# Modulation weights split between a merged first stage and the mLSTM: four blocks of 512 columns at the start, eight later

## The chip, the cores and the metric

One Trainium2 chip, one core of it. The metric is the device time of one execution in microseconds (us); 3 runs of the kernel before are given by their median. Lower is better. TensorE (PE) runs at one of two clock levels, 1.2 or 2.4 GHz; the profile gives the granted share (0.50 or 1.00, or a mean of them).

## What is computed

The reference is three transformer layers over 512 tokens of width 1024, all in fp32. Only the head of the first one matters here:

```python
mx = [t[:, None, :] for t in jnp.split(jax.nn.silu(c) @ w_ada[l] + b_ada[l], 6, axis=-1)]
mc = jnp.split(jax.nn.silu(c_ctx) @ w_ada[l] + b_ada[l], 6, axis=-1)
hx = _modulate(_rms_norm(x, g_pre_mix[l]), mx[0], mx[1])
hc = _modulate(_rms_norm(ctx, g_pre_mix[l]), mc[0], mc[1])
yx, yc = _token_mixer(hx, hc, w_in[l], b_in[l], ...)          # project_in, mLSTM, convolution, project_out
x = x + mx[2] * _rms_norm(yx, g_post_mix[l])
hx = _modulate(_rms_norm(x, g_pre_ffn[l]), mx[3], mx[4])
x = x + mx[5] * _rms_norm(_moe_ffn(hx, ...), g_post_ffn[l])
```

`w_ada` is 1024 x 6144, 24 MB. Its product with two vectors, silu(c) and silu(c_ctx), gives six modulation vectors of 1024 for each. The first two (4 of 12 blocks of 512 columns) are wanted before the token mixer, the other four (8 blocks) only behind it.

## The kernel before

The kernel is a row of stages, each an `nc.Block()` in which every engine has its own hand-written instruction stream, with semaphores between them; a barrier of all engines stands between stages. Buffers are opened and closed with the stages. The order is that of the code: no scheduler moves anything. All loads go through one hardware queue, issued by SyncE (SP).

`load_and_modulation` loads the small tensors, x (3 MB, tokens and context, 768 columns for each of 8 k-tiles) and the 12 blocks of `w_ada` (2 MB each) through two buffers. For a block, TensorE makes 8 matmuls (line 302) whose stationary operand is silu_c (128 x 2) and whose moving operand is 512 columns of the weights, so the result is a row of 2 x 512; ScalarE copies it (line 333), TensorE turns it into columns with 4 transposes (line 310), and VectorE adds the bias into `m.mod` (line 344). A fp32 matmul of the program is two MATMUL records in the trace, each with an LDWEIGHTS of its own; a transpose is one.

Then come `modulation_gain` (line 480), `rms_norm` (squares in line 381, mean by a matmul with a constant in line 402, root 384, reciprocal 410, scaling 416, shift 390), and `project_in`, whose SP stream issues the loads of `w_in` when the stage before it has ended (line 536).

`mlstm` has three parts. First VectorE and ScalarE make running sums of the gates, then TensorE spreads them over the partitions with `sel` (line 853, 8 rounds, K = 64 rows) and ScalarE copies them. Then come 16 units (4 heads x 4 tiles of 128 tokens), each with two directions. TensorE's order over a unit is: `qk` for the next unit (line 871), `turn` (transposes of the scores, line 882), `pv` of the previous direction (line 894), `turn`, `pv`. VectorE makes logits (805), the product with the decay (794) and the division (773 to 781). At the end VectorE normalizes over each head (826 to 838), and TensorE, which waits for that (`mixed`), turns the result (line 911).

```python
                for n in range(len(subs)):
                    if n % 2 == 0 and n // 2 + 1 < len(units):
                        qk(n // 2 + 1)
                    turn(n)
                    if n >= 1:
                        pv(n - 1)
```

Of the kernel before, what the change touches and what calls it, by code (L numbers as in the profile page):

```python
# [20 lines left out]
P = 128  # L21
D = 1024
# [240 lines left out]
        return stack, sb, sem  # L263


def load_and_modulation(m, d):

    nc, ps = m.nc, m.ps
    stack, sb, sem = m.open()
    N_AB = 6 * D // 512  # L270
    with stack:
        w = [sb(f"w_ada{s}", [P, KT, 512]) for s in range(2)]
        cs = sb("silu_c", [P, KT, 2])
        row = [sb(f"row{s}", [2, 512]) for s in range(2)]
        small_in, x_in, w_in = sem("small_in"), m.x_in, [sem("w_in0"), sem("w_in1")]
        silu_done, w_used, row_copied, turned, added, seen = (
            sem(s) for s in ("silu_done", "w_used", "row_copied", "turned", "added", "seen"))
        with nc.Block() as block:
            @block.sync
            def _(sp):  # L280
                sp.dma_start(m.vec[:], d["vec"]).then_inc(small_in, 16)
                for s in range(2):
                    sp.dma_start(w[s][:].rearrange("p k n -> p (k n)"), d["w_ada"][s]).then_inc(w_in[s], 16)
                sp.dma_start(m.const[:], d["const"]).then_inc(small_in, 16)
                sp.dma_start(m.rowv[:], d["rowv"]).then_inc(small_in, 16)
                sp.dma_start(m.x[:].rearrange("p k t -> p (k t)"), d["x"]).then_inc(x_in, 16)
                with sp.Fori(1, N_AB // 2) as g:
                    for s in range(2):
                        sp.wait_ge(w_used, 2 * g - 1 + s)
                        sp.dma_start(w[s][:].rearrange("p k n -> p (k n)"), d["w_ada"][2 * g + s]).then_inc(w_in[s], 16)  # L290
                sp.wait_ge(small_in, 48)
                sp.wait_ge(x_in, 16)

            @block.tensor
            def _(pe):
                ident = CONST.of(m.const, "ident")[0:2, 0:2]

                def product(n, s, loads):
                    pe.wait_ge(w_in[s], loads)
                    pe.wait_ge(row_copied, n + 1)  # L300
                    for k in range(KT):
                        mm = pe.matmul(ps[0:2, s, :], cs[:, k, :], w[s][:, k, :], start=(k == 0), stop=(k == KT - 1))
                    mm.then_inc(w_used, 1)

                def turn(n, s):
                    pe.wait_ge(row_copied, n + 3)
                    pe.wait_ge(added, n + 1)
                    pe.sem_inc(seen, 1)
                    for a in range(4):
                        mm = pe.transpose(ps[:, 2 + s, 2 * a:2 * a + 2], row[s][:, a * P:(a + 1) * P], ident)  # L310
                    mm.then_inc(turned, 1)

                pe.wait_ge(silu_done, 1)
                product(0, 0, 16)
                with pe.Fori(0, N_AB // 2 - 1) as g:
                    product(2 * g + 1, 1, 16 * g + 16)
                    turn(2 * g, 0)
                    product(2 * g + 2, 0, 16 * g + 32)
                    turn(2 * g + 1, 1)
                product(N_AB - 1, 1, 8 * N_AB)  # L320
                turn(N_AB - 2, 0)
                turn(N_AB - 1, 1)

            @block.scalar
            def _(act):
                act.wait_ge(small_in, 48)
                act.activation(cs[:].rearrange("p k c -> p (k c)"), VEC.of(m.vec, "c"), ACT.Silu).then_inc(silu_done, 1)
                act.sem_inc(row_copied, 2)
                with act.Fori(0, N_AB // 2) as g:
                    for s in range(2):  # L330
                        act.wait_ge(w_used, 2 * g + s + 1)
                        act.wait_ge(added, 2 * g + s + 1)
                        act.activation(row[s][:], ps[0:2, s, :], ACT.Copy).then_inc(row_copied, 1)

            @block.vector
            def _(dve):
                dve.sem_inc(added, 2)
                dve.wait_ge(small_in, 48)
                b_ada = VEC.of(m.vec, "b_ada")
                with dve.Fori(0, N_AB // 2) as g:  # L340
                    for s in range(2):
                        dve.wait_ge(turned, 2 * g + s + 1)
                        at = bass.ds(16 * g + 8 * s, 8)
                        dve.tensor_tensor(m.mod[:, at], ps[:, 2 + s, 0:8], b_ada[:, at], ALU.add).then_inc(added, 1)


class Split:
# [310 lines left out]
def mlstm(m, d, mix):  # L658
# [10 lines left out]
    with stack:  # L669
# [10 lines left out]
        cols = [sb(f"row_cols{i}", [P, 8, 2]) for i in range(4)]  # L680
        hout = sb("hout", [P, TT, D_ML])
        ss, rs = sb("ss", [P, TT * H_M]), sb("rs", [P, 2, TT * H_M])
        (sel_in, l_abs, l_exp, l_ln, own_s, run_done, rr_done, rr_copied, ac_done, ac_copied, qk_done, qk_free, t_done,
         p_done, s_done, tr_done, st_done, pv_done, h_done, thr_done, ss_done, rs_done, mixed, mt_done) = (
            sem(s) for s in ("sel_in", "l_abs", "l_exp", "l_ln", "own", "run_done", "rr_done", "rr_copied", "ac_done",
# [9 lines left out]
        with nc.Block() as block:  # L695
            @block.sync
            def _(sp):
                sp.dma_start(sel[:].rearrange("p a b n -> p (a b n)"), d["sel"]).then_inc(sel_in, 16)

            @block.scalar  # L700
            def _(act):
                act.wait_ge(l_abs, 1)
                act.activation(tmp[:], tmp[:], ACT.Exp, scale=-1.0).then_inc(l_exp, 1)
                act.wait_ge(l_exp, 1)
# [41 lines left out]
            def _(dve):  # L746
# [94 lines left out]
            def _(pe):  # L841
                pe.wait_ge(sel_in, 16)
# [55 lines left out]
                qk(0)  # L898
                for n in range(len(subs)):
# [1187 lines left out]
def program(nc, d, out, scratch):  # L2087
    stack = ExitStack()
    m = Machine(nc, stack)
    with stack:  # L2090
        _, sb, sem = m.open(stack)
        m.x_in = sem("x_in")
# [13 lines left out]
        def norm_gain(name, at):  # L2106
            return lambda k, g: VEC.of(m.vec, name, at + k, 1)

        load_and_modulation(m, d)
        modulation_gain(m, "g_pre_mix", 1)  # L2110
        s1, sb1, _ = m.open()
        with s1:
            mix = sb1("mix", [P, KT, SEQ])
            s2, sb2, _ = m.open()
            with s2:
# [2 lines left out]
                s3, sb3, _ = m.open()  # L2118
                with s3:
                    m.h = sb3("h", [P, KT, ALLT])  # L2120
                    rms_norm(m, m.x, m.h, [(0, SEQ), (SEQ, CTX)], gain, mod(0))
                    project_in(m, d, mix)
                mlstm(m, d, mix)
            y = sb1("y", [P, KT, SEQ])
# [59 lines left out]
```

## Time and profile before

| | |
|---|---|
| median of 3 runs | 3138.53 us (3136.46 to 3147.02) |
| profiled execution, its own time | 3144.45 us |
| span of that execution's trace | 3142.4 us |
| mean granted TensorE clock | 0.916 |
| PE busy, share of the span | 2616.0 us, 83% |
| PE weight loads busy | 1865.6 us, 59% |
| DVE busy | 1702.6 us, 54% |
| ACT busy | 1210.8 us, 39% |
| DMA moved | 418.73 MB, mean 133 GB/s |

The span runs from the first to the last instruction of the trace, and the execution's own time is 2.05 us longer. Busy shares are means over stages with different limits; the stages touched here are the first 500 us. PE is TensorE's matmuls, PEld its weight loads, DVE VectorE, ACT ScalarE, SPq the queue instructions of SyncE. Times in rows count from the span's start.

### The profile page before, as it was taken

Reading aid. Unit: us, or ns where it says so; the run is one execution under the profiler, and the core shown is the slowest. Engines: PE = TensorE matmul, PEld = TensorE weight load, DVE = VectorE, ACT = ScalarE, POOL = GpSimd, SP = SyncE. Lnnn points to the kernel's source line nnn. Section 1 sums busy time; section 2 is a strip of 40 time slices with the busy share of each in tenths; the row PEclk is TensorE's granted clock in tenths of the full one; section 3 lists DMA queues with packets and bytes.
Section 4 is the critical chain, followed back from the end, with each engine's and each line's share of the span. In section 5 each row is a group of like instructions: output and inputs, shape, how many; then the busy total and the mean of one; then the engine's idle time right before and its main releaser. Section 6 shows DMA issues by size and latency. Waiting matters only on the chain. (4 is left out here: it accounts for less than half of the span.)

```text
span 3142.4 us, 32477 instructions
## 1 busy us (share of the span) xinstructions
PE 2616.0 (83%) x11074; PEld 1865.6 (59%) x11074; DVE 1702.6 (54%) x2822; ACT 1210.8 (39%) x1922; POOL 182.0 (6%) x138
## 2 busy tenths in 40 slices
PE   7699787478999989985289986999958885689998
PEld 1244365336666666664167764888846663578886
DVE  0238385337777777775645534645534556455363
ACT  0200352217777776763223333523322222244232
POOL 0000000002222222221000000000000000000000
PEclk9899798679999999998599997999978997899999
DMA  7410001208999999985411111222211100132222
GB/s 293 160 73 1 4 1 54 104 32 312 328 329 326 324 318 318 323 318 216 164 54 40 40 54 65 96 94 94 91 63 41 60 20 1 53 120 91 97 89 72
DMA packets 103619, 418.73 MB, mean 133 GB/s; under 512 B 20240, under 2 KB 20368, under 8 KB 92752
## 3 DMA queue, kind: packets, MB, share of 16 engines
q1 hardware_dynamic: 84208, 383.68, 34.1%
q0 software_dynamic: 19296, 33.60, 3.1%
q8 instruction: 62, 1.02, 0.1%
q14 instruction: 53, 0.43, 0.0%
HBM read 415.10 MB, written 38.80 MB: 144 GB/s over the span
## 5 line engine op out<-in xcount | busy, mean ns | idle before, releaser
L1327 ACT ACTIVATE w_gu_high<-raw 128x1024 fp32r<-128x1024 f32 x264 | 279.7, 1060 | 113.2 <-PE banks L1283 112.3
L2000 PE MATMUL banks<-h_high,w_high 128*128 128x512 f32 x704 | 276.5, 393 | 48.9 <-DVE w_low L2054 48.9
L1386 DVE TENSOR_TENSOR w_gu_low<-raw,w_gu_high 128x1024 fp32r<-128x1024 f32 x264 | 310.9, 1217 | 4.2 <-ACT w_gu_high L1327 3.6
L2000 PE MATMUL banks<-h_low,w_high 128*128 128x512 f32 x704 | 276.0, 392 | 0.0
L2000 PE MATMUL banks<-h_high,w_low 128*128 128x512 f32 x704 | 275.9, 392 | 0.0
L1283 PE MATMUL banks<-w_gu_high,x_t_high 128*128 128x512 f32 x528 | 215.3, 408 | 35.4 <-DVE x_t_low L1397 35.4
L1283 PE MATMUL banks<-w_gu_high,x_t_low 128*128 128x512 f32 x528 | 208.3, 395 | 0.0
L1283 PE MATMUL banks<-w_gu_low,x_t_high 128*128 128x512 f32 x528 | 208.0, 394 | 0.0
L2054 DVE TENSOR_TENSOR w_low<-raw,w_high 128x2048 fp32r<-128x2048 f32 (+2 forms) x76 | 152.9, 2012 | 90.5 <-ACT w_high L2024 90.5
L2024 ACT ACTIVATE w_high<-raw 128x2048 fp32r<-128x2048 f32 (+2 forms) x76 | 127.9, 1684 | 177.7 <-PE banks L2010 157.8
L1476 POOL DMA_INDIRECT x_rows<-h_rows,token_i x68 | 110.5, 1625 | 1250.0 <-DVE token_i L1422 1231.6
L2000 PEld LDWEIGHTS banks<-h_high,w_high 128*128 128x128 f32 x704 | 133.5, 190 | 78.3 <-issue 50.6
L1658 PE MATMUL banks<-w_qkv,h 128*128 128x128 f32 x1024 | 133.2, 297 | 26.1 <-DVE k L1774 25.9
L2000 PEld LDWEIGHTS banks<-h_low,w_high 128*128 128x128 f32 x704 | 133.4, 190 | 27.7
L2000 PEld LDWEIGHTS banks<-h_high,w_low 128*128 128x128 f32 x704 | 133.3, 189 | 27.7
L1658 PEld LDWEIGHTS banks<-w_qkv,h 128*128 128x128 f32 x1024 | 130.1, 212 | 29.6 <-DVE k L1774 29.6
L2034 ACT ACTIVATE conv<-banks,vec 128x512 f32<-128x512 f32 x88 | 67.8, 771 | 200.8 <-PE banks L2000 200.8
L1297 PE MATMUL banks<-raw,act_t 128*128 128x512 f32 x264 | 137.5, 603 | 0.0
L2010 PE MATMUL banks<-hidden_high,w_high 128*128 128x512 f32 x352 | 137.4, 390 | 0.0
L2010 PE MATMUL banks<-hidden_high,w_low 128*128 128x512 f32 x352 | 137.1, 390 | 0.0
L2010 PE MATMUL banks<-hidden_low,w_high 128*128 128x512 f32 x352 | 137.1, 390 | 0.0
L1283 PEld LDWEIGHTS banks<-w_gu_high,x_t_high 128*128 128x128 f32 x528 | 99.9, 189 | 59.9 <-DVE x_t_low L1397 39.1
(320 smaller groups left out, 5035.6 us busy)
## 6 DMA issues: line engine op xcount, KB each, us to landing
raw<-in_w_e SPq DMA_DIRECT2D x396, 512.0 KB, 6.8
raw<-in_w_up SPq DMA_DIRECT2D x44, 1024.0 KB, 4.8
w_ada<-in_w_ada SPq DMA_DIRECT2D x12, 2048.0 KB, 8.0
expert_rows<-y_rows SPq DMA_DIRECT2D x16, 1024.0 KB, 11.3
w_qkv<-in_w_even SPq DMA_DIRECT2D x8, 1536.0 KB, 6.5
raw<-in_w_down SPq DMA_DIRECT2D x16, 768.0 KB, 4.2
w_qkv<-in_w_odd SPq DMA_DIRECT2D x8, 1536.0 KB, 6.5
raw<-in_w_down SPq DMA_DIRECT2D x16, 640.0 KB, 3.9
```

Source lines behind the costliest of these rows:

```text
L1283: mm = pe.matmul(ps[:, BG, :], xp[:, k, :], wp[:, j, :], start=(k == 0 and i == 0), stop=(k == KT - 1 and i == 2))
L1297: pe.matmul(ps[:, BY + n, :], at_f[:], raw[GU + 1][s][:, half], start=False, stop=True).then_inc(y_made, 1)
L1327: act.activation(w_gu[c].high[:].rearrange("p j n -> p (j n)"), raw[c][s][:], ACT.Copy).then_inc(gu_high, 1)
L1386: dve.tensor_tensor(w_gu[c].low[:].rearrange("p j n -> p (j n)"), raw[c][s][:], w_gu[c].high[:].rearrange("p j n -> p (j n)").bitcast(F32) ...
L1476: pool.indirect_dma_start(xg[s][:], None, scratch["h_rows"], bass.IndirectOffsetOnAxis(ap=token_i[s][:, 0:1], axis=0), bounds_check=SEQ - ...
L1658: mm = pe.matmul(ps[:, BP, i * P:(i + 1) * P], m.h[:, kk, i * P:(i + 1) * P], w[s][:, 2, kk, :], start=(kk == 0), stop=(kk == KT - 1))
L2000: mm = pe.matmul(ps[:, 2 * s + c, :], wp[:, at:at + P], hp[:, k, :], start=(k == 0 and i == 0), stop=(k == KT - 1 and i == 2))
L2010: mm = pe.matmul(ps[:, 4 + s, :], wp[:, k * P:(k + 1) * P], hp[:, k, :], start=(k == 0 and i == 0), stop=(k == b - a - 1 and i == 2))
L2024: act.activation(w[s].high[:, 0:cols], raw[s][:, 0:cols], ACT.Copy).then_inc(high_done, 1)
L2034: act.activation(y[s][:, c, :], ps[:, 2 * s + c, :], ACT.Identity, scale=tap(t, c, 2), bias=tap(t, c, 3)).then_inc(tap0, 1)
L2054: dve.tensor_tensor(w[s].low[:, 0:cols], raw[s][:, 0:cols], w[s].high[:, 0:cols].bitcast(F32), ALU.subtract).then_inc(low_done, 1)
```

## The change

The stages `load_and_modulation`, `modulation_gain` and `rms_norm` become one, `prologue`. It loads x in 8 pieces ahead of 4 blocks of `w_ada`, each in a buffer of its own, makes the norm's squares and mean as the pieces of x land, and then the 4 blocks. The products are made the other way round, there and in `mlstm`: the stationary operand is 128 x 128 of the weights and the moving one is silu_c with 2 columns, so that the result stands in columns at once; row copies and transposes are gone. The norm is scaled without the gain; gain and shift are applied last, on VectorE for the tokens and on ScalarE for the context. The other 8 blocks are loaded in `mlstm` through two buffers and computed there in 32 parts, a part being 128 of the weights' columns: 8 matmuls of the program.

```diff
+def prologue(m, d):
+    N_FIRST = 4
+    BA, BS = 0, 1
             @block.sync
             def _(sp):
+                sp.dma_start(m.vec[:], d["vec"]).then_inc(vec_in, 16)
+                sp.dma_start(m.const[:], d["const"]).then_inc(const_in, 16)
+                for k in range(KT):
+                    sp.dma_start(m.x[:, k, :], d["x"][:, k * ALLT:(k + 1) * ALLT]).then_inc(x_in[k], 16)
+                for n in range(N_FIRST):
+                    sp.dma_start(w[n][:].rearrange("p k n -> p (k n)"), d["w_ada"][n]).then_inc(w_in[n], 16)
+                sp.dma_start(m.rowv[:], d["rowv"]).then_inc(rowv_in, 16)
+                sp.wait_ge(rowv_in, 16)
             @block.tensor
             def _(pe):
-                ident = CONST.of(m.const, "ident")[0:2, 0:2]
-                def product(n, s, loads):
-                    for k in range(KT):
-                        mm = pe.matmul(ps[0:2, s, :], cs[:, k, :], w[s][:, k, :], start=(k == 0), stop=(k == KT - 1))
-                def turn(n, s):
...
+                pe.wait_ge(const_in, 16)
+                for k in range(KT):
+                    pe.wait_ge(sq_done, k + 1)
+                    for g, (t, n) in enumerate(groups):
+                        mm = pe.matmul(ps[:, BS + g, 0:n], CONST.of(m.const, "inv_d"), sq[:, k, t:t + n], start=(k == 0), stop=(k == KT - 1))
+                mm.then_inc(ms_done, 1)
+                pe.wait_ge(silu_done, 1)
+                for n in range(N_FIRST):
+                    pe.wait_ge(w_in[n], 16)
                     for a in range(4):
+                        t = 4 * n + a
+                        for k in range(KT):
+                            mm = pe.matmul(ps[:, BA, 2 * t:2 * t + 2], w[n][:, k, a * P:(a + 1) * P], cs[:, k, :],
+                                           start=(k == 0), stop=(k == KT - 1))
+                mm.then_inc(parts_done, 1)
             @block.scalar
...
+                for k in range(KT):
+                    act.wait_ge(x_in[k], 16)
+                    act.activation(sq[:, k, :], m.x[:, k, :], ACT.Square).then_inc(sq_done, 1)
...
+                act.wait_ge(gain_done, 1)
+                act.wait_ge(unit_done, KT)
+                for k in range(KT):
+                    act.activation(m.h[:, k, SEQ:], sq[:, k, SEQ:], ACT.Identity, scale=m.gain[:, k, 1:2], bias=mod[:, k, 1:2])
             @block.vector
             def _(dve):
+                dve.wait_ge(std_done, 2)
+                dve.reciprocal(std[:], std[:]).then_inc(rstd_done, 1)
+                dve.wait_ge(rstd_done, 1)
+                for k in range(KT):
+                    dve.tensor_tensor(sq[:, k, :], m.x[:, k, :], std[:], ALU.mult).then_inc(unit_done, 1)
+                dve.wait_ge(parts_done, 1)
...
+                dve.tensor_tensor(m.mod[:, at], ps[:, BA, at], VEC.of(m.vec, "b_ada")[:, at], ALU.add).then_inc(mod_done, 1)
...
+                for k in range(KT):
+                    dve.tensor_scalar(m.h[:, k, 0:SEQ], sq[:, k, 0:SEQ], m.gain[:, k, 0:1], mod[:, k, 0:1], ALU.mult, ALU.add)
@@ mlstm @@
                 sp.dma_start(sel[:].rearrange("p a b n -> p (a b n)"), d["sel"]).then_inc(sel_in, 16)
+                for n in range(N_LATER):
+                    if n >= 2:
+                        sp.wait_ge(aw_used, 4 * (n - 1))
+                    sp.dma_start(aw[n % 2][:].rearrange("p k n -> p (k n)"), d["w_ada"][N_ADA + n]).then_inc(aw_in[n % 2], 16)
...
             def _(act):
+                act.activation(cs[:].rearrange("p k c -> p (k c)"), VEC.of(m.vec, "c"), ACT.Silu).then_inc(cs_done, 1)
...
+                dve.wait_ge(aw_used, 4 * N_LATER)
+                dve.tensor_tensor(m.mod[:, 8 * N_ADA:], ps[:, BM, M_AT:M_AT + 8 * N_LATER], VEC.of(m.vec, "b_ada")[:, 8 * N_ADA:], ALU.add)
...
+                def later_part(t):
+                    n, a = divmod(t, 4)
...
+                    for k in range(KT):
+                        mm = pe.matmul(ps[:, BM, M_AT + 2 * t:M_AT + 2 * t + 2], aw[n % 2][:, k, a * P:(a + 1) * P], cs[:, k, :],
+                                       start=(k == 0), stop=(k == KT - 1))
+                    mm.then_inc(aw_used, 1)
+
                 pe.wait_ge(sel_in, 16)
+                for t in range(4):
+                    later_part(t)
                 pe.wait_ge(run_done, 1)
                 for n in range(2 * H_M):
...
                     mm.then_inc(rr_done, 1)
+                    if n % 2 == 1:
+                        later_part(4 + n // 2)
...
                 def pv(n):
                     h, i, r = subs[n]
                     k0, w = keys(i, r)
-                    pe.wait_ge(st_done, n + 1)
                     if n >= 2:
                         pe.wait_ge(h_done, n - 1)
+                    if n % 2 == 0:
+                        later_part(8 + n // 2)
+                    pe.wait_ge(st_done, n + 1)
...
                 pv(len(subs) - 1)
+                pe.wait_ge(h_done, len(subs))
+                for t in range(24, 32):
+                    later_part(t)
```

The next blocks are TensorE's instruction order, where a row is a matmul of the program with its output shape and a count. `banks` is PSUM; `w_ada_7` and `silu_c` are the operands of a part. First, TensorE in the second and third unit of `mlstm`, before (lines 871, 882 and 894 are `qk`, `turn` and `pv`):

```order
L871 MATMUL banks<-k,q 128x512 x2
L882 MATMUL banks<-const,scores_9 128x128 x5
L894 MATMUL banks<-v,scores_t_9 128x128 x5
L882 MATMUL banks<-const,scores_9 128x128 x4
L894 MATMUL banks<-v,scores_t_9 128x128 x5
```

The same place in the changed kernel, where `qk`, `turn` and `pv` are lines 898, 909 and 923:

```order
L898 MATMUL banks<-k,q 128x512 x2
L909 MATMUL banks<-const,scores_7 128x128 x5
L923 MATMUL banks<-v,scores_t_7 128x128 x5
L909 MATMUL banks<-const,scores_7 128x128 x4
L861 MATMUL banks<-silu_c,w_ada_7 128x2 x8
L923 MATMUL banks<-v,scores_t_7 128x128 x5
```

In each of the 16 units one part now stands between the second `turn` and the `pv` of the first direction. Second, TensorE at the end of `mlstm`, before; line 911 is the final turn of `hout`, and the rows behind it are the end of the stage and the start of `project_out`:

```order
L894 MATMUL banks<-v,scores_t_9 128x128 x4
L882 MATMUL banks<-const,scores_9 128x128 x3
L894 MATMUL banks<-v,scores_t_9 128x128 x9
L911 MATMUL banks<-const,hout 128x128 x16
L695 UNCONDITIONAL_BRANCH
```

And in the changed kernel:

```order
L923 MATMUL banks<-v,scores_t_7 128x128 x4
L909 MATMUL banks<-const,scores_7 128x128 x3
L861 MATMUL banks<-silu_c,w_ada_7 128x2 x8
L923 MATMUL banks<-v,scores_t_7 128x128 x9
L861 MATMUL banks<-silu_c,w_ada_7 128x2 x64
L943 MATMUL banks<-const,hout 128x128 x16
```

The last unit's part stands ahead of the last `pv`, and 64 matmuls, which are 8 parts, now stand between that `pv` and the final turn.

## Rows read from the trace of the kernel before

**Rows 1.** Windows: us, busy PE, PEld, DVE, ACT, POOL, granted clock, DMA share, GB/s

```profile
19.39:115.20 95.81, 90.91 (x240) 19.51 (x240) 2.00 (x12) 7.25 (x13) 0.00 (x0) 1.00 0.68 245
...
362.23:384.50 22.27, 21.78 (x49) 14.13 (x49) 0.00 (x0) 7.39 (x18) 0.00 (x0) 0.50 0.00 1
...
401.86:472.87 71.01, 63.19 (x374) 44.67 (x373) 65.21 (x240) 38.98 (x109) 0.00 (x0) 1.00 0.00 1
...
485.60:499.14 13.54, 0.00 (x0) 0.03 (x1) 12.26 (x55) 0.31 (x1) 0.00 (x0) 0.64 0.00 0
```

**Rows 2.** DMA issues of the first 28 us: KB each, median us to landing

```profile
x<-in_x SPq DMA_DIRECT2D x1, 3072.0 KB, 23.6
const<-in_const SPq DMA_DIRECT2D x1, 1217.5 KB, 15.3
...
vec<-in_vec SPq DMA_DIRECT2D x1, 349.5 KB, 3.9
```

**Rows 3.** Timeline of TensorE, 97 to 152 us: start, us, what

```profile
98.25 7.03 PE L302 MATMUL banks<-w_ada,silu_c 128*2 128x512 f32 x16
...
116.73 12.28 PE L402 MATMUL banks<-sq,const 128*128 128x512 f32 x32 [2.56 <-ACT sq L381]
151.75 101.53 PE L566 MATMUL banks<-h,w_in 128*128 128x512 f32 x256 [22.74 <-DMA w_in<-in_w_in]
```

**Rows 4.** Timelines of the other engines, 97 to 212 us, columns as in rows 3

```profile
115.31 0.24 DVE L480 SCALAR_TENSOR_TENSOR gain<-mod,vec 128x8 f32<-128x8 f32 x2 [0.79 <-PEq L254]
115.83 5.98 ACT L381 ACTIVATE sq<-x 128x768 f32<-128x768 f32 x8 [2.19 <-PEq L475]
...
142.56 0.89 ACT L390 ACTIVATE h<-sq,mod 128x256 f32<-128x256 f32 x2
144.15 2.38 SPq L536 DMA_DIRECT2D w_in<-in_w_in  x5
...
209.32 1.92 DVE L634 TENSOR_SCALAR mix<-u,vec 128x512 f32<-128x512 f32 x4
```

**Rows 5.** Matmuls with few moving columns: timeline of L1014, group of L1865

```profile
616.11 13.92 PE L1014 MATMUL banks<-w_router,h 128*128 128x64 f32 x64 [22.24 <-DMA ws_dn<-in_ws_dn]
...
L1865 PE MATMUL banks<-prod,const 128*128 128x2 f32 x2 | 0.6, 365 | 3.7 <-DVE prod L1857 3.7
```

**Rows 6.** Timeline of TensorE: first and last of 28 such matmuls

```profile
669.44 0.55 PE L1031 MATMUL banks<-mask,const 128*128 128x64 f32 x4
...
671.62 1.06 PE L1035 MATMUL banks<-mask,const 128*128 128x64 f32 x8
```

**Rows 7.** Windows around changes of the granted clock, columns as in rows 1

```profile
616.11:630.03 13.92, 13.92 (x65) 13.92 (x66) 0.00 (x0) 0.00 (x0) 0.00 (x0) 0.50 0.77 311
...
115.00:120.00 5.00, 3.27 (x6) 1.83 (x7) 0.24 (x2) 4.17 (x6) 0.00 (x0) 0.73 0.02 3
120.00:125.00 5.00, 5.00 (x16) 2.85 (x16) 0.00 (x0) 3.10 (x4) 0.00 (x0) 0.93 0.00 0
...
130.00:135.00 5.00, 0.00 (x0) 0.00 (x0) 5.00 (x4) 0.10 (x1) 0.00 (x0) 0.94 0.00 0
...
670.00:675.00 5.00, 2.67 (x24) 2.54 (x23) 2.12 (x7) 0.00 (x0) 0.00 (x0) 0.87 0.00 0
```

**Rows 8.** Timeline of the mLSTM: SyncE's only load in it

```profile
348.22 0.57 SPq L698 DMA_DIRECT2D sel<-in_sel  x1
```

**Rows 9.** Timeline of TensorE in the mLSTM, three parts of it

```profile
362.26 20.82 PE L853 MATMUL banks<-run,sel 64*128 64x256 f32 x40 [19.68 <-DVE run L765]
...
384.49 7.16 PE L871 MATMUL banks<-k,q 64*128 64x512 f32 x8 [0.46 <-ACT a_col L713]
...
482.80 2.06 PE L894 MATMUL banks<-v,scores_t 128*128 128x128 f32 x17
499.14 1.09 PE L911 MATMUL banks<-const,hout 128*128 128x128 f32 x4 [14.28 <-DVE hout L838]
```

**Rows 10.** Waits, 401.86 to 472.87 us (12 units): us, times, longest

```profile
PE banks L882 <- DVE row_cols L794: 7.1, 9, 1.1
```

More of the change, by code:

```diff
@@ L263, in open @@
         return stack, sb, sem
-def load_and_modulation(m, d):
+def prologue(m, d):
     nc, ps = m.nc, m.ps
     stack, sb, sem = m.open()
-    N_AB = 6 * D // 512
+    N_FIRST = 4
+    BA, BS = 0, 1
     with stack:
[L272 to L277, printed above, removed]
+        w = [sb(f"w_ada{n}", [P, KT, 512]) for n in range(N_FIRST)]
+        cs, sq = sb("silu_c", [P, KT, 2]), sb("sq", [P, KT, ALLT])
+        std = m.so[:].rearrange("p i n -> p (i n)")[:, 0:ALLT]
+        vec_in, const_in, rowv_in, w_in = sem("vec_in"), sem("const_in"), sem("rowv_in"), [sem(f"w_in{n}") for n in range(N_FIRST)]
+        x_in = [sem(f"x_in{k}") for k in range(KT)]
+        silu_done, sq_done, ms_done, std_done, rstd_done, unit_done, parts_done, mod_done, gain_done = (
+            sem(s) for s in ("silu_done", "sq_done", "ms_done", "std_done", "rstd_done", "unit_done", "parts_done", "mod_done", "gain_done"))
+        groups = [(0, SEQ), (SEQ, CTX)]
+        mod = m.mod[:].rearrange("p (j c) -> p j c", c=2)
         with nc.Block() as block:
@@ L280, in _ @@
             def _(sp):
[L281 to L290, printed above, removed]
@@ L294, in _ @@
+                sp.dma_start(m.rowv[:], d["rowv"]).then_inc(rowv_in, 16)
+                sp.wait_ge(rowv_in, 16)
             @block.tensor
             def _(pe):
-                ident = CONST.of(m.const, "ident")[0:2, 0:2]
-                def product(n, s, loads):
-                    pe.wait_ge(w_in[s], loads)
-                    pe.wait_ge(row_copied, n + 1)
-                    for k in range(KT):
-                        mm = pe.matmul(ps[0:2, s, :], cs[:, k, :], w[s][:, k, :], start=(k == 0), stop=(k == KT - 1))
-                    mm.then_inc(w_used, 1)
@@ L305, in turn @@
-                def turn(n, s):
-                    pe.wait_ge(row_copied, n + 3)
-                    pe.wait_ge(added, n + 1)
-                    pe.sem_inc(seen, 1)
-                    for a in range(4):
[L310 to L319, printed above, removed]
@@ L320, in _ @@
-                product(N_AB - 1, 1, 8 * N_AB)
-                turn(N_AB - 2, 0)
-                turn(N_AB - 1, 1)
+                pe.wait_ge(const_in, 16)
[5 more added lines that the diff above has]
+                pe.wait_ge(silu_done, 1)
@@ L324, in _ @@
+                for n in range(N_FIRST):
+                    pe.wait_ge(w_in[n], 16)
+                    for a in range(4):
+                        t = 4 * n + a
[3 more added lines that the diff above has]
+                mm.then_inc(parts_done, 1)
             @block.scalar
             def _(act):
-                act.wait_ge(small_in, 48)
+                act.wait_ge(vec_in, 16)
@@ L327, in _ @@
                 act.activation(cs[:].rearrange("p k c -> p (k c)"), VEC.of(m.vec, "c"), ACT.Silu).then_inc(silu_done, 1)
[L328 to L333, printed above, removed]
+                for k in range(KT):
+                    act.wait_ge(x_in[k], 16)
+                    act.activation(sq[:, k, :], m.x[:, k, :], ACT.Square).then_inc(sq_done, 1)
@@ L335, in _ @@
+                act.wait_ge(ms_done, 1)
+                for g, (t, n) in enumerate(groups):
+                    act.activation(std[:, t:t + n], ps[:, BS + g, 0:n], ACT.Sqrt, bias=CONST.of(m.const, "eps")).then_inc(std_done, 1)
+                act.wait_ge(gain_done, 1)
+                act.wait_ge(unit_done, KT)
+                for k in range(KT):
+                    act.activation(m.h[:, k, SEQ:], sq[:, k, SEQ:], ACT.Identity, scale=m.gain[:, k, 1:2], bias=mod[:, k, 1:2])
             @block.vector
@@ L336, in _ @@
             def _(dve):
[L337 to L344, printed above, removed]
+                dve.wait_ge(std_done, 2)
@@ new lines, in _ @@
+                dve.reciprocal(std[:], std[:]).then_inc(rstd_done, 1)
[3 more added lines that the diff above has]
+                dve.wait_ge(parts_done, 1)
+                dve.wait_ge(vec_in, 16)
+                at = slice(0, 8 * N_FIRST)
+                dve.tensor_tensor(m.mod[:, at], ps[:, BA, at], VEC.of(m.vec, "b_ada")[:, at], ALU.add).then_inc(mod_done, 1)
@@ new lines, in _ @@
+                dve.wait_ge(mod_done, 1)
+                for c in range(2):
+                    ins = dve.scalar_tensor_tensor(m.gain[:, :, c], mod[:, KT:2 * KT, c], 1.0, VEC.of(m.vec, "g_pre_mix"),
+                                                   ALU.add, ALU.mult)
+                ins.then_inc(gain_done, 1)
+                dve.wait_ge(gain_done, 1)
+                dve.wait_ge(unit_done, KT)
+                for k in range(KT):
+                    dve.tensor_scalar(m.h[:, k, 0:SEQ], sq[:, k, 0:SEQ], m.gain[:, k, 0:1], mod[:, k, 0:1], ALU.mult, ALU.add)
@@ L682, in mlstm @@
         ss, rs = sb("ss", [P, TT * H_M]), sb("rs", [P, 2, TT * H_M])
+        aw, cs = [sb(f"w_ada{s}", [P, KT, 512]) for s in range(2)], sb("silu_c", [P, KT, 2])
+        aw_in, aw_used, cs_done = [sem("w_ada_in0"), sem("w_ada_in1")], sem("w_ada_used"), sem("silu_c_done")
+        BM, M_AT, N_ADA, N_LATER = 6, DV, 4, 8
         (sel_in, l_abs, l_exp, l_ln, own_s, run_done, rr_done, rr_copied, ac_done, ac_copied, qk_done, qk_free, t_done,
@@ L838, in _ @@
                     dve.tensor_tensor(hout[:, i, :], hout[:, i, :], m.so[:, i, :], ALU.mult).then_inc(mixed, 1)
+                dve.wait_ge(aw_used, 4 * N_LATER)
+                dve.tensor_tensor(m.mod[:, 8 * N_ADA:], ps[:, BM, M_AT:M_AT + 8 * N_LATER], VEC.of(m.vec, "b_ada")[:, 8 * N_ADA:], ALU.add)
             @block.tensor
             def _(pe):
+                def later_part(t):
+                    n, a = divmod(t, 4)
+                    if t == 0:
+                        pe.wait_ge(cs_done, 1)
+                    if a == 0:
+                        pe.wait_ge(aw_in[n % 2], 16 * (n // 2) + 16)
+                    for k in range(KT):
+                        mm = pe.matmul(ps[:, BM, M_AT + 2 * t:M_AT + 2 * t + 2], aw[n % 2][:, k, a * P:(a + 1) * P], cs[:, k, :],
+                                       start=(k == 0), stop=(k == KT - 1))
+                    mm.then_inc(aw_used, 1)
                 pe.wait_ge(sel_in, 16)
+                for t in range(4):
+                    later_part(t)
                 pe.wait_ge(run_done, 1)
@@ L2090, in program @@
     with stack:
-        _, sb, sem = m.open(stack)
-        m.x_in = sem("x_in")
+        _, sb, _ = m.open(stack)
         m.ps = stack.enter_context(nc.psum_tensor("banks", [P, 8, 512], F32))
@@ L2120, in program @@
                     m.h = sb3("h", [P, KT, ALLT])
-                    rms_norm(m, m.x, m.h, [(0, SEQ), (SEQ, CTX)], gain, mod(0))
+                    prologue(m, d)
                     project_in(m, d, mix)
```

4 lines of the change are left out of this document (removed).

## The prediction

> **What bounds the kernel now.** I read the windows first, then the timeline of each engine in the first 500 us, and then the waits. The first stage is bound by its own chain of 2 MB loads through two buffers, one block of matmuls and the next load: TensorE is busy for 90.91 of 95.81 us at the high level, and the DMA share is only 0.68 [rows 1]. Then the norm runs with no DMA at all, and the loads of the next stage are issued when it has ended, at 144.15 [rows 4]; TensorE has its first matmul of that stage at 151.75 [rows 3]. That is 7.6 us for 2,048 KB. So everything up to 144.15 lies on the path, and what a shorter start saves is whole.
>
> In the mLSTM the path goes through TensorE while it spreads the sums: 20.82 us without a gap [rows 9], at the low level throughout (0.50) [rows 1]. In the 12 units from 401.86 to 472.87 one takes 5.92 us. There DVE is the bound: 65.21 of 71.01 us busy, and TensorE, 63.19 busy at 1.00, waits 7.1 us for it [rows 1, 10], so TensorE has 0.65 us to spare in a unit. At the end it waits 14.28 us for the normalized heads [rows 9].
>
> **The change part by part.** The unit of the sum is what one record costs when 128 x 128 weights are loaded for few columns. The nearest row is L1014: 64 records with 64 columns in 13.92 us, at 0.50 throughout [rows 5, 7]. Less the first one's lead that is 0.214 us each. At the high level 28 like them run from 669.44 to 672.68 [rows 6]; less the modelled tail of the last, 0.28, that is 0.11 each. With 2 columns there are only the two records of L1865: union 0.6, mean 0.365, so they start 0.235 apart, after an idle engine and at the low level [rows 5]. So fewer columns don't make it cheaper. I take 0.214 and 0.11. A block is 4 x 8 x 2 = 64 records: 13.7 us low, 7.0 high, against 7.03 before for 16 records with 512 columns [rows 3]. A part is 3.4 or 1.8.
>
> Which level holds? L1014 kept TensorE busy for 13.92 us and the clock never rose [rows 7]. So nearly all blocks and parts that stand by themselves are paid at the low level.
>
> *Prologue.* The first five loads were 9.76 MB in one queue; x alone took from rowv's landing at 19.4 to its own at 26.7, 3.15 MB or 431 GB/s [rows 2]. vec lands at 4.6, const near 7.7, the 8 pieces of x 0.92 us apart, the last near 15.2; the four blocks near 20, 25, 30 and 35. (The Trainium skill, "DMA: Bandwidth & Descriptors", section "Bandwidth", gives a 1 MB transfer 341 GB/s and asks for pieces of 1 MB or more; by it the pieces of x would cost some 2 us more, as an estimate, all under TensorE's matmuls of the mean.) ScalarE's squares, 8 in 5.98 us [rows 4], keep up. The 32 records of the mean took 12.28 us with a low stretch at their start [rows 3, 7]; from 9.4 they end near 22. Then 256 records: 54.9 us low, less 3.4 for the few us in which the clock is still high, so they end near 73.5, long after the last load and the norm's reciprocal and scaling (some 14 us on DVE behind 22). Then mod, two gains (0.24), 8 scalings (4 take 1.92) beside 8 on ScalarE (2 take 0.89) [rows 4], hops and the barrier: 5.3 us. The stage ends at 78.8, which saves 144.15 - 78.8 = 65.3. Bounds: everything low and late 61, the high level throughout 90.
>
> *mLSTM, start.* sel is issued at 348.22 [rows 8]; the first block behind it lands 8.8 us later (7.6 as w_in's, 0.6 for sel, 0.6 to issue), at 357.0. Four parts at the low level end at 370.7, but L853 started at 362.26 [rows 9]: +8.4. What is late is every copy of ScalarE and then the first unit.
>
> *Between the 8 rounds:* 4 parts in TensorE's gapless 20.82 us, with K = 64 at 0.50 before [rows 1]: +13.7.
>
> *Units.* At the high level a part adds 1.76 to 5.27 busy (63.19/12), so TensorE, with 7.0, becomes the bound, and a unit grows by 1.1: 17.6 for 16. Behind the part stands `pv`, for whose result DVE waits, and behind it the next `qk`. The units start at the low level (0.50 up to 384.5 [rows 1]), and parts prolong it: +5.6, of which 1.6 is the first part at the low price and 4 a guess for the rest. And the clock may fall in a unit. It fell at about 673.7 (0.87 over 5 us), 1 us after 28 records with few columns, but at about 134.4 and 489.4 only some 5 us after fuller work had ended, at 129.0 and 484.9 [rows 1, 3, 7, 9]: such records seem to count for little, so a part of 1.8 us in 7 is close to what makes it fall. The short dip at 115 to 125 lasted 3.4 us (0.27 x 5 + 0.07 x 5, doubled) and cost half of that [rows 7]; I take two falls of twice this length, +7. Together +30. Bounds: the part half hidden, 0.6 a unit, +10; all at the low level, where a unit is 3.4 (qk, 8 records in 7.16 [rows 9]), 5.8 (27 of turn and pv at 0.214) and 3.4, 12.6 in place of 5.92: +107.
>
> *End.* 8 parts are 27.4 us low, less 2.7 for a clock still high at first. From 485.6 they end at 510.3 in place of 499.14 [rows 9]: +11.2. Bounds: +1 (all high), +14.
>
> ScalarE's silu (0.2 us) lies under its idle time, the last addition on DVE behind the final turn. The later loads wait for parts that are two blocks back, tens of us ahead.
>
> Sum: -65.3 + 8.4 + 13.7 + 30 + 11.2 = -2.0. The profiled execution took 3144.45 with a span of 3142.4; it stands 5.9 above the median of 3138.53. So 3142.5 for such an execution, and **3137 us** as a median.
>
> **The rivals.** A: *the clock holds in the units* and the parts fit better, C = 10 to 20 in place of 30: 3117 to 3128, say 3122. For it: 1.00 over 71 us although TensorE waits [rows 1]. Chance 0.28.
>
> B: *the clock falls in the units.* One mechanism: a part adds idle-like time, the clock drops, the unit takes 12.6, and rises only where turn and pv are dense. One fall of 3.4 us' cost in every unit gives 54 in place of 7: 3184; all low: 3214. It decides from three more falls on (over 9.4 us). For it: the fall at 673.7 and the low level of L1014. Against: a part is only a quarter of the unit. Chance 0.28.
>
> C: *a weight load at half the price.* If a record with 2 columns cost half of L1014's, 0.107, at either level, the prologue would end 24 us earlier (its loads end at 35), each group of four parts cost 6.9 less, the end 11 less: 3137 - 49 = 3088. Against it the 0.235 of L1865 [rows 5]. The Trainium skill, "TensorE: Matmul & The Clock Gate", section "LDWEIGHTS (loading the stationary operand)", has loading take the number of columns over 1.2 GHz, 107 ns here; by that rule the time is this rival's. The trace disagrees where the weights are fp32: 0.214 low and 0.11 high. Chance 0.06.
>
> **How the numbers follow.** The forecast, all terms within some 9 us of the sum, 0.38, its own range 3128 to 3147. Faster and slower start at 0.3%, 9.4 us, about what a measurement of this kernel can tell from no change. Faster: A and C, 0.34. Same: 0.38. Slower: B, 0.28. The range leaves out C and the far half of B: 3108 to 3178.
>
> **What would show it.** First load of w_in at 77 to 81 and the 256 records 50 to 55 us long, at 0.50. L853's group 8 us after DVE's last run sum, and near 34 us long with its parts. Units of 6.9 to 7.1 where the granted clock is 1.00. The final turn 24 us behind the last `pv`. Wrong would make it: records 0.11 apart at 0.50 (C), or a granted share under 0.8 over the 16 units (B).

## The result, and the profile after

The changed kernel takes 3153.44 us (median of 20 runs, 3145.39 to 3162.95), the kernel before 3139.67 us (20 runs, 3135.44 to 3149.18). The ratio is 1.0043, with a 95% interval of 1.0033 to 1.0052: slower by 13.8 us, where 2 us less, counted as no change, was forecast. The time lies inside the predicted range, but on the side that had a chance of 0.28.

The profiled execution has a span of 3152.3 us, against 3142.4, and TensorE's share rises although the product of the modulation is no larger: 2683.6 us of matmuls against 2616.0.

```profile
span 3152.3 us, 33281 instructions
...
PE 2683.6 (85%) x11602; PEld 1994.7 (63%) x11602; DVE 1703.8 (54%) x2811; ACT 1198.3 (38%) x1903; POOL 182.4 (6%) x138
```

The windows of the changed kernel by stage (columns: us, busy time and instructions of each engine, granted clock, DMA share, GB/s): the first stage, `project_in`, the mLSTM, and then four stretches of the mLSTM.

```profile
0.00:79.70 79.70, 65.35 (x288) 59.53 (x288) 16.20 (x21) 14.61 (x21) 0.20 (x4) 0.66 0.43 176
79.70:287.00 207.30, 192.70 (x452) 82.72 (x452) 103.50 (x149) 19.53 (x27) 0.00 (x0) 0.95 0.13 51
287.00:523.00 236.00, 222.74 (x1072) 179.49 (x1072) 109.80 (x389) 66.79 (x173) 0.00 (x0) 0.67 0.20 73
...
346.90:369.90 23.00, 22.20 (x64) 14.47 (x65) 10.53 (x37) 7.46 (x18) 0.00 (x0) 0.50 0.20 83
369.90:455.30 85.40, 85.22 (x428) 65.60 (x427) 49.58 (x182) 28.32 (x83) 0.00 (x0) 0.72 0.14 50
455.30:492.40 37.10, 36.51 (x264) 30.36 (x263) 26.32 (x101) 16.50 (x46) 0.00 (x0) 1.00 0.20 65
...
492.40:518.00 25.60, 24.78 (x130) 24.72 (x129) 12.97 (x58) 0.31 (x1) 0.00 (x0) 0.57 0.17 72
```

Three of these rows (346.90 to 492.40) are the units: the same work at three clocks, 0.50 at the start, 0.72 over 85 us in which TensorE is busy for 85.22, and 1.00 at the end. Before, 12 of 16 units ran at 1.00 without a break [rows 1]. The 0.72 is a mean of the two levels. Below are the 16 units as a whole, whose share before was 0.94, and one of the stretches at the low level in them:

```profile
346.90:492.40 145.50, 143.93 (x752) 110.43 (x752) 86.42 (x317) 52.29 (x146) 0.00 (x0) 0.76 0.16 59
...
373.34:380.17 6.83, 6.83 (x25) 4.81 (x23) 3.09 (x11) 1.77 (x5) 0.00 (x0) 0.50 0.00 0
```

The prediction's sign for B, a granted share under 0.8 over the 16 units, has come: 0.76.

The timeline of TensorE shows the places of the sum:

```profile
9.09 13.46 PE L300 MATMUL banks<-sq,const 128*128 128x512 f32 x32 [9.09 <-ACT sq L318]
22.39 52.05 PE L308 MATMUL banks<-silu_c,w_ada 128*128 128x2 f32 x256
...
296.07 13.79 PE L861 MATMUL banks<-silu_c,w_ada 128*128 128x2 f32 x64 [14.63 <-DMA w_ada<-in_w_ada]
309.79 5.48 PE L878 MATMUL banks<-run,sel 64*128 64x256 f32 x12
315.20 3.57 PE L861 MATMUL banks<-silu_c,w_ada 128*128 128x2 f32 x16
...
397.37 1.84 PE L861 MATMUL banks<-silu_c,w_ada 128*128 128x2 f32 x16
399.08 0.91 PE L923 MATMUL banks<-v,scores_t 128*128 128x128 f32 x6
399.92 3.10 PE L898 MATMUL banks<-k,q 64*128 64x512 f32 x4
...
472.04 1.98 PE L898 MATMUL banks<-k,q 64*128 64x512 f32 x4
...
493.29 24.83 PE L861 MATMUL banks<-silu_c,w_ada 128*128 128x2 f32 x128 [0.82 <-DVE hout L791]
```

The 4 records of `qk` (L898) show the clock in each unit: 1.98 us at the high level, 3.78 at the low, 3.10 where the level changes under them. From 399.92 the next three `qk` start at 410.26, 420.60 and 430.94, 10.3 us apart; at 1.00 two are 7.06 apart (472.04 and 479.10).

The differences by stage, barrier to barrier, in the two profiled executions: first stage 79.7 for 144.0 (-64.3), `project_in` 207.3 for 204.1 (+3.2), mLSTM 236.0 for 156.0 (+80.0), all behind it -9.0. The sum is +9.9, the difference of the spans. Of the last figure -5.5 is one stage, the experts (762.1 for 767.6), and in the profiles of this case that stage, which no edit touches, takes 758.3 to 767.6; `project_in` takes 203.9 to 207.3. So most of both is scatter between executions. The medians differ by 13.8.

The mLSTM by the prediction's own cuts: start (stage's start to the first round) +8.7, rounds 37.1 for 22.2 (+14.9), units (first `qk` to the last `pv`) 145.5 for 100.4 (+45.2), end 25.5 for 14.3 (+11.2).

### The profile page after: what moved, and what is told of

It reads as the page before. It is cut to its first block and busy times, and to the rows that moved or that the text cites. A ratio compares the mean times of both kernels' runs of the same rounds, so it can differ in the third digit from the quotient of the medians.

```text
span 3152.3 us, 33281 instructions
## 1 busy us (share of the span) xinstructions
PE 2683.6 (85%) x11602; PEld 1994.7 (63%) x11602; DVE 1703.8 (54%) x2811; ACT 1198.3 (38%) x1903; POOL 182.4 (6%) x138
```

## The experiments

All are edits of the changed kernel. The quantities to compare are the stage mLSTM and, in it, the time from the first `qk` to the last `pv` ("the units"): 100.4 us before, 145.5 changed.

### More moving columns in the mLSTM: 128 and 64

```diff
-        ..., sb("silu_c", [P, KT, 2])
+        ..., sb("silu_c", [P, KT, 128])
+                dve.memset(cs[:, :, 2:], 0.5).then_inc(cs_done, 1)
-                        mm = pe.matmul(ps[:, BM, M_AT + 2 * t:M_AT + 2 * t + 2], aw..., cs[:, k, :], ...)
+                        mm = pe.matmul(ps[:, BM, M_AT + 2 * t:M_AT + 2 * t + 128], aw..., cs[:, k, :], ...)
```

A part writes its two results and 126 columns behind them; the part after it writes over these from its own two columns on, so no result that counts is lost. "T" and "O" are the two explanations that the expectations compare. With 128:

> The later parts' matmuls (stage mLSTM) get 128 moving columns in place of 2; the 126 new ones are a constant and only the first two of each result are kept, so the output is the same. The two theories: T, records with 2 columns count for little, and so TensorE's clock falls once in each unit; O, the parts cost what TensorE's occupation costs, and the clock falls for another reason (waits for DVE). T expects: records as dear as before at a given level (0.11 high, 0.21 low), units near 7.0 us at a granted clock of 1.00, so the 145.5 us from the last round to the last pv become about 118; the end 25.5 becomes 15 to 17; the start 1 to 4 us shorter; the rounds, 37.1, between 20 and 37. In all 40 to 55 us less than the changed kernel: 3100 to 3115. O expects the falls to stay: units near 10 us, 3150 to 3160. A third, that a record's columns come on top of its weight load (0.21 + 0.21 low), expects some 3210.

Measured: 3091.32 us (median of 4 runs), ratio to the kernel before 0.9851, interval 0.9826 to 0.9876. The stage is 173.7 us, the units 116.0. The windows of the units, and TensorE at the end, with 128 columns:

```profile
326.00:442.00 116.00, 113.92 (x752) 89.78 (x752) 86.37 (x318) 52.36 (x146) 0.00 (x0) 0.97 0.21 75
```

```profile
436.33 1.06 PE L924 MATMUL banks<-v,scores_t 128*128 128x128 f32 x8
437.64 0.52 PE L910 MATMUL banks<-const,scores 128*128 128x128 f32 x3 [0.25 <-ACT scratch L734]
438.00 1.95 PE L862 MATMUL banks<-silu_c,w_ada 128*128 128x128 f32 x16
...
442.78 14.56 PE L862 MATMUL banks<-silu_c,w_ada 128*128 128x128 f32 x128 [0.82 <-DVE hout L792]
```

The same 752 records, each with 64 times the columns where it is a part, take 29.5 us less. A part costs 1.95 at the high level where it cost 1.84 with 2 columns, so the columns are almost free beside the weight load, and the clock is high with them. T holds; O and the theory that columns come on top fall. The whole gain, 62, is more than T's 40 to 55, since the rounds gained as much as T had thought possible (305.79 to 325.96, 20.2 us for 37.1).

> As the run with 128 moving columns, with 64. T, where columns count by their number, expects that a half does less: a level between, part of the units at about 7.0 us and part near 10, the end (8 parts alone) again at the low level near 25 us; stage mLSTM between that of 128 columns (some 190 us) and that of the changed kernel (236). If only the presence of moving work counted, it would equal the run with 128. O expects 236.

Measured: 3113.96 us (one run), stage 202.8, units 123.7, between the two, as T says. But the place is not where T put it: the start, the rounds and the first 23 us of the units are at the low level as with 2 columns, while the rest of the units, and the 8 parts at the end, expected low, hold the high one without a fall. TensorE's first four parts with 64 columns, then the windows of the rounds, the units from 364 on, and the end:

```profile
289.92 13.88 PE L862 MATMUL banks<-silu_c,w_ada 128*128 128x64 f32 x64 [14.68 <-DMA w_ada<-in_w_ada]
```

```profile
303.70:339.80 36.10, 36.10 (x105) 26.63 (x104) 0.00 (x0) 6.98 (x16) 0.00 (x0) 0.50 0.16 59
...
364.00:465.00 101.00, 99.71 (x692) 80.35 (x690) 76.14 (x282) 44.93 (x128) 0.00 (x0) 1.00 0.19 66
465.00:480.30 15.30, 14.50 (x130) 14.50 (x131) 12.93 (x57) 0.31 (x1) 0.00 (x0) 1.00 0.28 119
```

### The same work at a finer or coarser grain, 2 columns

```diff
-                        mm = pe.matmul(ps[:, BM, ...], ..., start=(k == 0), stop=(k == KT - 1))
+                        mm = pe.matmul(ps[:, BM + k // 4, ...], ..., start=(k % 4 == 0), stop=(k % 4 == 3))
...
-                    if n % 2 == 0:
-                        later_part(8 + n // 2)
+                    later_part(8 + n // 2, range(4 * (n % 2), 4 * (n % 2) + 4))
```

> Columns stay at 2. Each part in a unit is cut in two halves of 8 records (the k-tiles 0 to 3 ahead of one pv, 4 to 7 ahead of the next; they add up in two PSUM banks, with one more addition at the end), so TensorE's work is the same and the longest stretch of few-column records is half as long (0.9 us at the high level). If the length of the stretch made the clock fall, the units would go back to 7.0 us and stage mLSTM to about 205 us. If the share of few-column work in a unit does it, the stage stays at 230 to 240 us with a fall in most units. O expects 236.

Measured: 3130.3 us (one run), stage 213.3, units 121.3. TensorE's timeline over one unit with halves, and two windows, of that unit and of the one behind it:

```profile
375.75 1.98 PE L900 MATMUL banks<-k,q 64*128 64x512 f32 x4
377.67 0.87 PE L911 MATMUL banks<-const,scores 128*128 128x128 f32 x6
378.38 0.95 PE L862 MATMUL banks<-silu_c,w_ada 128*128 128x2 f32 x8
379.19 1.14 PE L924 MATMUL banks<-v,scores_t 128*128 128x128 f32 x8
380.17 0.49 PE L911 MATMUL banks<-const,scores 128*128 128x128 f32 x3
380.49 0.95 PE L862 MATMUL banks<-silu_c,w_ada 128*128 128x2 f32 x8
381.31 1.58 PE L924 MATMUL banks<-v,scores_t 128*128 128x128 f32 x12
382.82 1.98 PE L900 MATMUL banks<-k,q 64*128 64x512 f32 x4
```

```profile
375.75:382.82 7.07, 7.07 (x51) 5.70 (x50) 5.14 (x22) 2.68 (x8) 0.00 (x0) 1.00 0.00 0
382.82:388.99 6.17, 6.17 (x43) 4.81 (x42) 5.27 (x19) 3.07 (x10) 0.00 (x0) 1.00 0.33 84
```

From 368.69 on each of the 13 `qk` takes 1.98 us: no fall is left, though the records of a unit are the same. The window of the units from 367 on:

```profile
367.00:464.70 97.70, 97.62 (x687) 79.59 (x686) 75.67 (x282) 45.45 (x128) 0.00 (x0) 1.00 0.18 66
```

So the share of few-column work in a unit doesn't decide alone; how densely it stands matters. The stage is 8 us longer than the expected 205: the units still start with 23 us at the low level, and the end takes 27.3.

The opposite, two parts in every second unit (`if n % 4 == 0:` and two calls):

> Columns stay at 2, and the same 16 parts run in the units, but as two in every second unit: 32 records, 3.7 us at the high level, without other work. The mean share of few-column work is the same as with one part or two halves a unit. T, in the form that the halves have left (what counts is how much other work lies around a stretch of such records), expects the clock to fall in each of these 8 pairs, and some units at the low level behind them: units together longer than with one part each, the 145.5 us from the last round to the last pv at 145 to 165. If only the mean share counted, 3153 and a stage of 236 as before, and the halves' gain would have come from another thing in them (two banks, the cut).

Measured: 3156.61 us (one run), stage 237.2, units 146.0. Behind most pairs a `qk` takes 3.78 us and the next one 1.98: the clock falls with the pair and rises in the unit without one. That is as T says, but the times decide nothing: T's range began at 145, and the rival, that only the mean share counts, expected 3153 and 236, as close to what was measured. It takes the control for the halves, in which the halves of two parts stand together in every second unit (`if n % 4 < 2:` and two calls with the same ranges), to decide:

> A control for the run with halves: columns stay at 2, the same two PSUM banks, the same cut of each part and the same last addition, but the halves of two parts stand together: 16 records ahead of each of the two pv of every second unit, none in the units between. So the stretches of few-column records are again as long as in the changed kernel (1.8 us at the high level), with some 2 us of other work between the two of a unit. T, that it is how densely such records stand at one place, expects the clock to fall in these units as in the pairs, and 140 to 152 us from the first qk to the last pv. If the two banks or the cut had made the units of the halves fast, it would be 121 us, as there.

Measured: 3146.05 us (one run), stage 230.9, units 141.0 at a granted clock of 0.80. With the same banks, cut and addition, falls are back where 16 records stand in a row. TensorE's timeline of this kernel around one of them, and the windows of the two falls:

```profile
391.30 1.84 PE L862 MATMUL banks<-silu_c,w_ada 128*128 128x2 f32 x16
393.00 1.54 PE L926 MATMUL banks<-v,scores_t 128*128 128x128 f32 x6
394.48 3.78 PE L900 MATMUL banks<-k,q 64*128 64x512 f32 x4
398.19 1.11 PE L911 MATMUL banks<-const,scores 128*128 128x128 f32 x4
399.09 3.41 PE L862 MATMUL banks<-silu_c,w_ada 128*128 128x2 f32 x16
```

```profile
393.10:406.70 13.60, 13.60 (x51) 10.83 (x51) 4.98 (x19) 2.49 (x7) 0.00 (x0) 0.50 0.00 0
457.90:471.60 13.70, 13.70 (x52) 10.82 (x50) 5.57 (x21) 3.12 (x11) 0.00 (x0) 0.50 0.00 0
```

These two, of some 14 us each, are all the falls behind the start of the units (the low level there lasts 29.0 us, for 23.5 in the halves); the other such units keep 1.00, and the units are 4.5 us shorter than in the changed kernel. Of the 19.7 us that they take over the halves' 121.3, the falls and the longer start are 16 (half of 27.3 and of 5.5), and 3 are longer waits of TensorE. It is one run, and why some fall and others don't stays open. No load was under way in either fall (the last two columns), while the halves' units held 1.00 with 66 GB/s: the loads don't make the clock fall.

### The parts out of the units

```diff
-                    if n % 2 == 0:
-                        later_part(8 + n // 2)
...
-                for t in range(24, 32):
+                for t in range(8, 32):
```

> The 16 parts in the units move to the end of the stage, where then 24 parts stand by themselves. T expects the units back at 5.92 us with a granted clock of 1.00 from where it rises on, the 145.5 us from the last round to the last pv back at 100 to 102 (-44), and the end 25.5 + 16 x 3.41 = 80 (+54.6): stage mLSTM 246 us, in all 10 us more than the changed kernel, about 3163. If something else than the parts had slowed the units (the loads that run meanwhile, buffers at other places), the units would stay above 6.5 us and the stage be near 270 us.

Measured: 3156.24 us (one run), stage 245.1, units 100.3, what they were before. So the buffers at other places cost the units nothing. Of the loads this run says little, since a load waits for the parts two blocks back: the loads now run at the start and the end of the stage, and from 360 to 443.4 there is almost none (1 GB/s). That the loads are harmless is shown by the halves, above. The tail's window, 24 parts alone:

```profile
444.00:523.40 79.40, 79.22 (x385) 79.22 (x386) 12.36 (x55) 0.31 (x1) 0.00 (x0) 0.52 0.29 106
```

### The first stage, and both together

The first stage's records get 128 columns in the same way (the tile lies in a free part of `m.so`):

> Only the first stage's 256 records get 128 moving columns in place of 2 (126 of them a constant whose results are overwritten or not read; the output is the same). T, few columns count for little, expects TensorE's clock to rise a few us after the mean's records end, and the 256 records 28.5 us at 0.11 each plus some us at the low level, 30 to 34, in place of 52.05; they would then end near 56, so the stage, 79.7 before, ends near 58 to 62: 18 to 22 us less in all, 3131 to 3137, with the mLSTM as in the changed kernel (236). The rival that the records are slow at any level because their weights are as good as all they load expects 52 and no gain. One that the stage waits for its loads expects none either: they end near 35.

Measured: 3138.11 us (median of 10), ratio 0.9986, interval 0.9972 to 1.0000. The windows of the 256 records, with 2 columns and with 128:

```profile
22.39:74.44 52.05, 52.05 (x257) 51.96 (x255) 11.99 (x9) 1.05 (x2) 0.00 (x0) 0.53 0.25 107
```

```profile
22.00:50.70 28.70, 28.70 (x257) 28.53 (x255) 11.99 (x9) 1.05 (x2) 0.00 (x0) 1.00 0.49 207
...
322.40:474.40 152.00, 150.16 (x752) 115.12 (x752) 86.44 (x318) 52.37 (x146) 0.00 (x0) 0.72 0.15 56
```

The records take 28.75 us, the stage 56.0 for 79.7. The high level never ended in them: not even the few us at the low one came that were expected. The profile also shows what I hadn't expected: the mLSTM, not touched, takes 242.2 us for 236.0, its units 152.0 for 145.5. The clock falls at other places and for longer: behind the start there are three stretches of 20.5 us at the low level, where the changed kernel has seven of 6.8. One of them:

```profile
361.90:382.40 20.50, 20.50 (x70) 14.97 (x69) 8.45 (x31) 4.55 (x13) 0.00 (x0) 0.50 0.28 103
```

So in this profile 6 of the 23.7 us were given back there, the median lies 1 us above the expected 3131 to 3137, and neither the number nor the length of the falls is fixed for the same code in `mlstm`. Whether that goes with the time at which the units begin, or differs from one execution to the next, one profile of each can't tell.

The halves on top of this test whether their high level was luck of their start:

> 128 moving columns in the first stage, halves with 2 columns in the mLSTM: the same work as in the run with 128 columns in the first stage alone, but for the cut. T expects the units at 1.00 whatever their place in time, 121 us from the first qk to the last pv in place of 151.9, and the stage mLSTM at 213 in place of 242: about 3110, 25 to 31 us less than that run's 3138. If the high level in the units of the halves had been luck of where they began, some 145 us and 3130 to 3140.

Measured: 3103.56 us (median of 4), ratio 0.9895, interval 0.9861 to 0.9930; stage mLSTM 210.2, units 120.8 at 0.91. The units began 20 us earlier than in the run with halves and took the same time, with every `qk` from 347.98 on at 1.98 us: the high level was not luck. The gain on the run with 128 columns in the first stage alone is 34.6 us in the medians, some more than the 25 to 31 expected.

> 128 moving columns in the first stage and in the mLSTM: if the two are independent, their gains add up, 62 us from the mLSTM and 18 to 22 from the first stage, so 3069 to 3075, 2.1 to 2.3% less than the kernel before. If the one's clock feeds on the other's place in time, some us to either side; a sum under 70 us off the changed kernel would say that they share something.

Measured: 3065.64 us (median of 5), ratio 0.9769, interval 0.9745 to 0.9793, so 2.3% less than the kernel before and 87.8 us less than the changed one, 3 us more of a gain than expected. The stages show 56.1 and 173.5 us, 23.6 and 62.5 less. This is the best version of the study. Its windows, the first stage, the mLSTM, its units and its end:

```profile
0.00:56.10 56.10, 41.48 (x288) 35.84 (x288) 17.09 (x22) 14.62 (x21) 0.20 (x4) 0.99 0.62 249
262.90:436.40 173.50, 159.65 (x1072) 130.54 (x1072) 110.61 (x390) 66.62 (x173) 0.00 (x0) 0.94 0.27 99
301.70:417.70 116.00, 113.93 (x752) 89.72 (x752) 86.37 (x317) 52.43 (x146) 0.00 (x0) 0.97 0.21 76
417.70:433.00 15.30, 14.48 (x130) 14.45 (x130) 12.93 (x58) 0.31 (x1) 0.00 (x0) 1.00 0.29 120
```

The 8 parts at the end now lie almost wholly under DVE's last work: the final turn comes 15.2 us behind the last `pv`, for 14.3 before.

## Why the prediction was wrong

**The step that failed** is in the term of the units, +30: "I take two falls of twice this length, +7". Measured, the units grew by 45.2, and the experiments split it.

- What the parts cost at the high level: put at the full clock, the halves' units take 121.3 less half of their 23.5 us at the low level, 109.5; those before take 100.4 less half of their 12.7, 94.0. That is 15.5 us for 16 parts. Predicted 17.6; right.
- The low level at their start: half of (23.5 - 12.7) is 5.4 us. Predicted 5.6; right.
- The falls behind it: 145.5 - 121.3 = 24.2 us in the changed kernel, and 31 in the profile of the run with 128 columns in the first stage alone (152.0). Predicted 7.

The two low stretches used here:

```profile
384.49:397.20 12.71, 11.95 (x25) 6.21 (x26) 8.15 (x27) 5.94 (x14) 0.00 (x0) 0.50 0.00 0
...
343.50:367.00 23.50, 22.72 (x67) 14.97 (x67) 11.04 (x38) 7.56 (x19) 0.00 (x0) 0.50 0.20 80
```

The window from 369.9 to 455.3 has 0.72 of the clock over 85.4 us, so 48 us of it at the low level (0.28 x 2 x 85.4). In the trace that is seven falls of about 6.8 us, each costing half of that, 3.4. In this execution the price of a fall was right to a tenth; their number was 7 and not 2. The prediction had written down the reason itself ("such records seem to count for little, so a part of 1.8 us in 7 is close to what makes it fall") and then given the falls by guess. That the reason was right was partly luck: it was read from a fall behind 28 records with 64 columns, and with 64 columns in `mlstm` 14.5 us of such records leave the clock at 1.00. For 2 columns the runs bear it out. Rival B was this mechanism; it was said to decide from three more falls on, and five more came. It had a fall in every unit, 3184 us, which was too many: of the 15 parts behind the start 7 are followed by a fall, and the last units, with the same work, hold the high level for 37 us. What decides which part is followed by one, no run shows; and the other 19 runs of the changed kernel have no trace here, so their falls aren't counted.

**The other terms.** Price of a record: 0.214 and 0.11 were taken, 256 of them took 52.05 (54.9 - 3.4 = 51.5 predicted), 64 took 13.79 (13.7), a part 3.57 or 1.84 with its tail (3.4, 1.8). The first stage ends at 79.7 (78.8 predicted): the mean's records end 0.5 us later than forecast, and the 256 behind them take 0.5 longer. The start +8.7 (8.4), the rounds +14.9 (13.7), the end +11.2 (11.2). The 3.2 us of `project_in` were in no term; six other profiles of kernels with the same first stage show 203.9 to 206.8 (a mean of 205.7), so about half of it is scatter, and 1 to 2 us may be real; I didn't test that.

**Rival C**, half the price at either level, is refuted at the low one: 64 records took 13.79 us with 2 columns, 0.215 each, and 13.88 with 64. Its 0.107 is close to the price at the high level alone, where 256 records took 28.75 us, 0.112 each. **Rival A**, that the clock holds and the units fit better, put the whole term of the units at 10 to 20. The halves measured +20.9, just beyond that, and 3130.3, not 3122. It needed stretches half as long.

**The sum** was -2.0. With the falls at 24 in place of 7 it is +15, against +13.8 in the medians; the other misses (first stage +1.0, start +0.3, rounds +1.2, the rest of the units -2.0) nearly cancel. The rest of the growth of 80 us in the mLSTM was foreseen, and so was the saving of the first stage.

The deeper cause is one for both stages: all 12 blocks now go through TensorE as weights for 2 columns, and where such records stand by themselves the clock goes to half. Of the stage's 80 us, 62 go with the columns alone. The Trainium skill, "TensorE: Matmul & The Clock Gate", section "Why this matters for your kernels", asks for a TensorE that is kept busy, to have the full clock. In this trace it was busy without a gap for 52.05 us, and the granted clock was 0.53: busy, in the sense of the profile, is not enough.

## What to carry to other kernels

A matrix times two vectors can go through TensorE with the matrix as weights, which saves the turning of the result, but in these runs TensorE's clock then dropped as if it idled, and slowed the work around it too. Give the moving operand more columns, even useless ones: here 126 constant columns cost 0.1 us in 1.8, and made the whole 2.3% faster than before, where the bare change was 0.4% slower. Where that can't be done, cut such work small and spread it between full matmuls. And when a forecast says "close to what makes the clock fall" inside a loop, count the falls by the iterations, not by a fixed number.

## What the runs showed of the hardware

- The weight load sets the pace of an fp32 record at 128 x 128: 16 records take 3.57 us at the low level with 2 columns and 3.67 with 64, and 1.84 (2 columns), 1.90 (64) and 1.95 (128) at the high one.
- Records of 64 columns kept the level at which they began, at both places where that can be seen. At the start of the mLSTM 64 of them and all the rounds stayed at 0.50 for over 40 us; at its end 128 of them ran 14.5 us at 1.00. With 2 columns alone the level fell, with 128 it rose or stayed high.
- Eight records with 2 columns between `turn` and `pv` left the clock at 1.00 in every unit behind the start, in two profiles. Behind sixteen at the same place it fell in 7 of 15 cases in the changed kernel, for 6.8 us each, three times for 20.5 us with an earlier start, and twice for 13.7 us where sixteen stood ahead of each `pv` of every second unit.
- The untouched stages scatter between the profiles of this case: the experts 758.3 to 767.7 us, `project_in` 203.9 to 207.3, the first stage of kernels with 2 columns 76.7 to 80.2 us.
